# Full-width tiles in a gated linear attention, a bias table written in two steps, and three reorderings around product-key experts

## The reference, cut to what matters

```python
def peer_ffn(h, w_q, sub_keys, expert_u, expert_v):     # 8 heads x 16 experts a token, 2 blocks of 128 tokens
    q = (hb @ w_q).reshape(128, 8, 2, 128)
    s = jnp.einsum('thpc,hpkc->thpk', q, sub_keys)
    top_s, top_i = lax.top_k(s, 16)
    cand_s = top_s[:, :, 0, :, None] + top_s[:, :, 1, None, :]     # 256 candidates
    fin_s, fin_pos = lax.top_k(cand_s.reshape(128, 8, 256), 16)
    idx = take_along_axis(cand_i, fin_pos); gates = softmax(fin_s)
    act = gelu(einsum('thkd,td->thk', expert_u[idx], hb))
    return einsum('thk,thkd->td', gates * act, expert_v[idx])

# second model, layer 0; 4 heads, keys of 96, values of 192
q, k, v, g, lr, mq = split_cols(xn @ gla_w_in, (384, 384, 768, 768, 16, 256))
main = gla_mixer(q, k, v, log_a, g, out_norm)   # ... rmsnorm_2(o, out_norm) * silu(g), per head over its 192
mo = mem_attention(mq, mem_kv)
h = h + concatenate([main, mo]) @ w_out         # 768 + 256 rows
# layer 1: tbl[rel_bucket(dist)], a bias by distance for each of 12 heads
```

## Time and profile before

| | us |
|---|---|
| median of 3 runs | 1646.41 |
| lowest, highest | 1645.17, 1646.71 |
| the profiled execution | 1647.83 |
| its span, first to last instruction | 1646.0 |
| TensorE busy | 1518.2 (92%) |
| VectorE busy | 938.1 (57%) |
| ScalarE busy | 414.1 (25%) |
| GpSimd busy | 597.7 (36%) |

### The profile page before, as it was taken

The page is one execution under the profiler, slowest core; times in us unless marked ns, Lnnn a source line. Parts: engine busy times, 40 slices in busy tenths (PEclk is TensorE's granted clock), DMA queues, the critical chain, the costliest instruction groups (busy, mean ns, idle before and its releaser), DMA issues. The chain is left out here.

```text
span 1646.0 us, 22237 instructions
## 1 busy us (share of the span) xinstructions
PE 1518.2 (92%) x7776; PEld 1138.2 (69%) x7778; DVE 938.1 (57%) x2383; ACT 414.1 (25%) x1007; POOL 597.7 (36%) x524
## 2 busy tenths in 40 slices
PE   7999989999999777778799999999999999999998
PEld 6998845554455323223357788999998878799997
DVE  5652576666766876766454732555553134555554
ACT  2120223213322222222124421111122145311112
POOL 4860233434333444434333103555521000455551
PEclk9999999999999999999999999999999999999999
DMA  8467699999999999999964135654424310555431
GB/s 326 162 224 158 244 428 387 427 426 427 427 420 426 423 427 427 427 426 397 426 282 153 52 128 219 213 169 162 153 106 133 121 52 1 205 169 168 162 127 38
DMA packets 64056, 421.70 MB, mean 256 GB/s; under 512 B 7456, under 2 KB 7904, under 8 KB 18432
## 3 DMA queue, kind: packets, MB, share of 16 engines
q0 software_dynamic: 38944, 277.19, 41.5%
q1 hardware_dynamic: 25024, 143.40, 24.3%
HBM read 416.12 MB, written 3.45 MB: 255 GB/s over the span
## 5 line engine op out<-in xcount | busy, mean ns | idle before, releaser
L2085 PE MATMUL wide<-arena 128*128 128x512 f32 x1024 | 475.4, 611 | 94.9 <-ACT arena L651 94.6
L2085 PEld LDWEIGHTS wide<-arena 128*128 128x128 f32 x1024 | 190.4, 193 | 357.4 <-issue 195.6
L1373 DVE CUSTOM_DVE_ANT_0 arena<-arena,wide 128x1024 f32<-128x1024 f32 x256 | 312.3, 1220 | 175.4 <-DMA arena<-uv_dram,arena 170.5
L494 POOL DMA_INDIRECT arena<-uv_dram,arena x256 | 260.0, 1016 | 406.1 <-PE wide L2085 288.4
L651 ACT ACTIVATE arena<-arena 128x2 f32<-128x2 f32 (+4 forms) x205 | 72.2, 354 | 507.1 <-DVE arena L1373 388.1
L2312 PE MATMUL wide<-arena,wring 128*128 128x256 f32 x704 | 158.6, 379 | 0.0
L1578 DVE SCALAR_TENSOR_TENSOR arena<-arena,prm 128x255 f32<-128x255 f32 (+1 forms) x152 | 126.0, 850 | 55.6 <-ACT arena L651 55.5
L2312 PEld LDWEIGHTS wide<-arena,wring 128*128 128x128 f32 x704 | 130.9, 190 | 16.2
L1612 DVE TENSOR_TENSOR arena<-bank,arena 128x128 f32<-128x128 f32 x266 | 73.9, 290 | 105.1 <-PE bank L2272 101.5
L651 ACT ACTIVATE arena<-bank 128x128 f32<-128x128 f32 (+7 forms) x102 | 41.7, 409 | 347.0 <-PE bank L2272 104.4
L505 POOL TENSOR_TENSOR arena<-arena 128x512 f32<-128x512 f32 x15 | 20.2, 1347 | 298.2 <-ACT arena L651 297.5
(11 more groups left out here) (275 smaller groups left out, 2126.4 us busy)
## 6 DMA issues: line engine op xcount, KB each, us to landing
wring<-ffn_dram SPq DMA_DIRECT2D x44, 1024.0 KB, 5.1
wring<-ffn_dram SPq DMA_DIRECT2D x44, 512.0 KB, 3.5
wring<-win_dram SPq DMA_DIRECT2D x15, 1024.0 KB, 5.4
wring<-wout_dram SPq DMA_DIRECT2D x8, 1024.0 KB, 9.3
wring<-wq_dram SPq DMA_DIRECT2D x5, 1024.0 KB, 7.5
wring<-wout_dram SPq DMA_DIRECT2D x4, 1280.0 KB, 5.5
wring<-mix_dram SPq DMA_DIRECT2D x4, 1024.0 KB, 5.3
arena<-uv_dram,arena POOLq DMA_INDIRECT x256, 11.8
```

What stands on the lines that cost most here:

```text
L494: pool.indirect_dma_start(out=G[:, n % NBUF, :], out_offset=None, in_=a["uv"], in_offset=bass.IndirectOffsetOnAxis(ap=idx[:, u, r:r + 1], ...
L1373: V.tensor_tensor_reduce(out=G[:, n % NBUF, 0:D], in0=G[:, n % NBUF, 0:D], in1=wide[:, 0:2, :].rearrange("p a b -> p (a b)"), scale=1.0, s ...
L2085: ins = MM(wide[:, 2 + h, :], diag[:, n % 4, e, :], G[:, r % NBUF, D + 512 * h:D + 512 * (h + 1)], start=r % (HEADS * TOPK) == 0, stop=r % ...
```

## The change

Six edits in one.

- Tiles. Queries and keys are packed as 3 slots of 2 x 128 columns: tile h holds head h's 96 and 32 of the fourth head's; VectorE copies the fourth head's parts to their partitions (for `gla_qk0` in two operations ahead of its scaling, for the others in four after the scans), and `gla_p0` waits for VectorE's copies. Values and gates are reordered as 4 tiles with the first 128 of each head and 2 tiles that hold the last 64 of two heads each. `glag` has 3 slots, `wout0` 8 row tiles instead of 10, and `gla_v0` stands ahead of `gla_p0`. The roots of the mean squares go from PSUM to `rinv` (ScalarE), the reciprocal is taken there.
- `wout0` runs the first four row tiles over all four groups, then the rest group by group.
- The bias table is written 8 times over (of 128) and copied on in memory by a second transfer; GpSimd waits for three.
- `wout` waits for the mixed tiles one by one.
- Unit 0's index is decoded in two halves (`select_in_halves`), and gathers 0 to 7 wait for the first only.
- `exps(1)` goes to pair 5 of unit 0, `exps(2)` ahead of `keep_head`, `exps(u + 2)` ahead of the eviction in a unit's last pair; some evictions move a pair later.

```diff
-          ("memkv", 4, 2048), ("glalr", 1, 128), ("glaqk", 4, 1536), ("glamq", 1, 2048), ("glav", 2, 3072), ("glag", 4, 1536),
-          ("wout0", 4, 2560), ("ffn0", FT, 3072), ("kvc", 2, 2048), ("nsamq", 1, 2048), ("nsagl", 1, 288), ("nsaq", 3, 2048), ("kvs", 4, 2048),
+          ("memkv", 4, 2048), ("glalr", 1, 128), ("glaqk", 3, 2048), ("glamq", 1, 2048), ("glav", 2, 3072), ("glag", 3, 2048),
+          ("wout0", 4, 2048), ("ffn0", FT, 3072), ("kvc", 2, 2048), ("nsamq", 1, 2048), ("nsagl", 1, 288), ("nsaq", 3, 2048), ("kvs", 4, 2048),
...
-          ("gla_gate", 2, ACT_), ("mean_fin", 1, DVE_), ("gla_qk1", 3, ACT_), ("gla_p0", 2, DVE_), ("gla_v0", 1, ACT_), ("gla_mq", 1, ACT_), ("gla_p1", 2, DVE_),
+          ("gla_gate", 2, ACT_), ("mean_fin", 1, DVE_), ("gla_qk1", 2, DVE_), ("gla_v0", 1, ACT_), ("gla_p0", 2, DVE_), ("gla_mq", 1, ACT_), ("gla_p1", 2, DVE_),
...
-          ("gla_ms", 2, DVE_), ("gla_g2", 1, ACT_), ("gla_g3", 1, ACT_), ("wout0", 4, DVE_),
+          ("gla_ms", 2, ACT_), ("gla_g2", 1, ACT_), ("wout0", 4, DVE_),
...
-                pool.wait_ge(idx_ready, u + 1)
+                pool.wait_ge(idx_ready, u + 2 if u else 1)
...
+                    if n == TOPK // 2:
+                        pool.wait_ge(idx_ready, 2)
+                        pool.sem_inc(fence["pool"])
...
-            pool.dma_start(a["turned"],
-                           tb[:, 512:896].unsqueeze(1).broadcast_to([12, 128, 384])).then_inc(bias_dram, 16)
+            pool.dma_start(a["turned"][:, 0:8, :], tb[:, 512:896].unsqueeze(1).broadcast_to([12, 8, 384])).then_inc(bias_dram, 16)
...
+            turned = a["turned"].tensor
+            pool.dma_start(bass.AP(turned, 8 * 384, [[128 * 384, 12], [8 * 384, 15], [1, 8 * 384]]),
+                           bass.AP(turned, 0, [[128 * 384, 12], [0, 15], [1, 8 * 384]])).then_inc(bias_dram, 16)
+            pool.wait_ge(bias_dram, 48)
...
+                    exps(2)
+                elif u == 1 and p == 2:
...
-                    exps(2)
-                elif 1 <= u <= 4 and p == 4:
+                elif 1 <= u <= 4 and p == 5:
...
+                    if u == 0 and p == 5:
+                        exps(1)
+                    elif u and p == PAIRS - 1 and u + 2 < UNITS:
+                        exps(u + 2)
...
-                if u + 2 < UNITS:
-                    exps(u + 2 if u else 1)
...
-            copy(gq[:, 2:4, :], halves(full("gla_qk1", 0), DK), scale=float(DK) ** -0.5).then_inc(freed[ACT_], 1)
-            copy(gk[:, 0:2, :], halves(full("gla_qk1", 1), DK)).then_inc(freed[ACT_], 1)
+            b = full("gla_qk1", 0)
+            copy(gq[:, 2, :], b[0:DK, 0:S], scale=float(DK) ** -0.5)
+            copy(gk[:, 0, :], b[0:DK, S:2 * S]).then_inc(qk_kept, 1)
+            copy(gk[:, 1:3, :], halves(full("gla_qk1", 1), DK)).then_inc(qk_kept, 1)
...
+            keep_v(0)
...
-            copy(gk[:, 2:4, :], halves(full("gla_qk1", 2), DK)).then_inc(freed[ACT_], 1)
...
-            keep_v(0)
...
-                copy(sqC[0:DK, 4 * n:4 * n + 4, :], wide[0:DK, 2 * n:2 * n + 2, :].rearrange("p a (b t) -> p (a b) t", b=2),
+                copy(sqC[:, 4 * n:4 * n + 4, :], wide[:, 2 * n:2 * n + 2, :].rearrange("p a (b t) -> p (a b) t", b=2),
...
-                root("gla_ms", i, DK, 2 * S)
+                copy(rinv.rearrange("p (q i) t -> p i q t", i=2)[:, i], halves(full("gla_ms", i)), func=ACT.Sqrt, bias=eps[:]).then_inc(freed[ACT_], 1)
...
-            keep_g(3)
...
+            def decode(q):
+                e = slice(8 * q, 8 * q + 8)
+                oh = [onehot[:, p, :].rearrange("p (k i) -> p k i", k=16)[:, e, :] for p in range(2)]
+                steps(V.tensor_scalar(pij[:, 0, e], pos[:, e], 4, 15, ALU.logical_shift_right, ALU.bitwise_and))
+                steps(V.tensor_scalar(pij[:, 1, e], pos[:, e], 15, 15, ALU.bitwise_and, ALU.bitwise_and))
+                join()
+                for p in range(2):
+                    steps(V.tensor_tensor(oh[p], pij[:, p, e].unsqueeze(2).broadcast_to([128, 8, 16]),
+                                          C("iota", 16).unsqueeze(1).broadcast_to([128, 8, 16]), ALU.is_equal))
+                join()
+                for p in range(2):
+                    steps(V.tensor_tensor(oh[p], oh[p], tif[:, p, :].unsqueeze(1).broadcast_to([128, 8, 16]), ALU.mult))
+                join()
+                for p in range(2):
+                    steps(V.tensor_reduce(eij[:, p, e], oh[p], X, ALU.add))
+                join()
+                V.scalar_tensor_tensor(out=idx[:, 0, e], in0=eij[:, 0, e], scalar=float(NKEYS), in1=eij[:, 1, e],
+                                       op0=ALU.mult, op1=ALU.add).then_inc(idx_ready, 1)
+            def select_in_halves():
+                for step in range(5):
+                    select(0, step)
+                flat, flat_w = cand.rearrange("p a b -> p (a b)"), cw.rearrange("p a b -> p (a b)")
+                join()
+                steps(V.max_index(pos[:, 0:8], fs[:, 0, 0:8], flat))
+                join()
+                decode(0)
+                steps(V.match_replace(flat_w, fs[:, 0, 0:8], flat, -3.0e38))
+                select(0, 6)
+                select(0, 7)
+                join()
+                decode(1)
...
-            for step in range(13):
-                select(0, step)
+            select_in_halves()
...
+            for m in range(2):
+                V.scalar_tensor_tensor(out=gq[32 * m:32 * m + 32, 3, :], in0=b[DK:128, m * S:(m + 1) * S], scalar=float(DK) ** -0.5,
+                                       in1=rstd[DK:128, :], op0=ALU.mult, op1=ALU.mult)
...
+            b = full("gla_qk1", 0)
+            dve.wait_ge(qk_kept, 1)
+            V.tensor_scalar(gq[64:DK, 3, :], b[DK:128, 0:S], float(DK) ** -0.5, None, ALU.mult)
+            V.tensor_copy(gk[0:32, 3, :], b[DK:128, S:2 * S]).then_inc(freed[DVE_], 1)
+            b = full("gla_qk1", 1)
+            dve.wait_ge(qk_kept, 2)
+            V.tensor_copy(gk[32:64, 3, :], b[DK:128, 0:S])
+            V.tensor_copy(gk[64:DK, 3, :], b[DK:128, S:2 * S]).then_inc(freed[DVE_], 1)
...
-                    dve.wait_ge(freed[ACT_], TAKEN[GROUP0["gla_qk1"] + 2])
+                    dve.wait_ge(freed[DVE_], TAKEN[GROUP0["gla_qk1"] + 1])
...
-                b = full("gla_ms", h // 2)
-                if h % 2 == 0:
-                    norm.n += 1
-                    dve.wait_ge(rooted, norm.n)
-                steps(V.reciprocal(rinv[:, h, :], b[0:DK, (h % 2) * S:(h % 2 + 1) * S]))
+                lo = 64 * (h % 2)
+                dve.wait_ge(freed[ACT_], TAKEN[GROUP0["gla_ms"] + h % 2])
+                steps(V.reciprocal(rinv[:, h, :], rinv[:, h, :]))
...
-                steps(V.tensor_tensor(gout[:, 2 * h:2 * h + 2, :], wide[0:DK, h, :].rearrange("p (b t) -> p b t", b=2),
-                                      rinv[:, h, :].unsqueeze(1).broadcast_to([DK, 2, S]), ALU.mult))
-                if h % 2:
-                    dve.drain().then_inc(freed[DVE_], 1)
-            steps.join()
-            for h in range(GH):
-                dve.wait_ge(freed[ACT_], TAKEN[GROUP0[f"gla_g{h}"]])
-                for v in range(2):
-                    j = 2 * h + v
-                    ins = V.scalar_tensor_tensor(out=gout[:, j, :], in0=gout[:, j, :], scalar=P("out_norm", v, rows=DK),
-                                                 in1=gg[:, j, :], op0=ALU.mult, op1=ALU.mult)
-                ins.then_inc(g_out, 1)
+                steps(V.tensor_tensor(gout[:, h, :], wide[:, h, 0:S], rinv[:, h, :], ALU.mult))
+                steps(V.tensor_tensor(gout[lo:lo + 64, 4 + h // 2, :], wide[lo:lo + 64, h, S:2 * S], rinv[lo:lo + 64, h, :], ALU.mult))
+                dve.wait_ge(freed[ACT_], TAKEN[GROUP0[f"gla_g{h // 2}"]])
+                steps.join()
+                V.scalar_tensor_tensor(out=gout[:, h, :], in0=gout[:, h, :], scalar=P("out_norm", 0), in1=gg[:, h, :],
+                                       op0=ALU.mult, op1=ALU.mult).then_inc(g_out, 1)
+            dve.wait_ge(freed[ACT_], TAKEN[GROUP0["gla_g2"]])
+            for j in range(4, 6):
+                V.scalar_tensor_tensor(out=gout[:, j, :], in0=gout[:, j, :], scalar=P("out_norm", 1), in1=gg[:, j, :],
+                                       op0=ALU.mult, op1=ALU.mult).then_inc(g_out, 1)
...
-            pe.wait_ge(mixed, 8)
-            def tokens(w, src, b, t, ms=(0, 1), norms=None):
+            def tokens(w, src, b, t, ms=(0, 1), norms=None, mixes=False):
...
+                        if mixes and m == 0:
+                            pe.wait_ge(mixed, k + 1)
...
-                done(tokens(slot("wout", i), mT, b, 0))
+                done(tokens(slot("wout", i), mT, b, 0, mixes=i == 0))
...
-                    lead("gla_qk0", b, slot("glaqk", 0), DK, p // 2 - 1, 0)
+                    lead("gla_qk0", b, slot("glaqk", 0), 128, p // 2 - 1, 0)
...
-                ins = lead("gla_qk0", bank[GROUP0["gla_qk0"] % 4], slot("glaqk", 0), DK, m, 1)
```

(69 more changed lines are left out.)

31 lines of the change are left out of this document (17 added, 14 removed).

## The result

| us | before | after |
|---|---|---|
| median of 7 runs each, taken together | 1646.71 | 1635.61 |
| lowest, highest | 1645.17, 1657.36 | 1631.17, 1637.11 |
| the profiled execution | 1647.83 | 1635.63 |
| its span | 1646.0 | 1633.8 |

The ratio is 0.9899, 95% interval 0.9872 to 0.9926: 1.0%, or 17 us (12 to 21) of the time before. By the medians the gain is 11.1 us, by the profiled executions 12.2. Forecast were 23.6 us and 1622.8 us. The sign and the mechanism were right; the size was not. The median of 1635.61 lies 5 us above the stated range; by the ratio, on the 1646.41 us that the forecast started from, it is 1629.8, just inside it.

A forecast was written before the change was run, and what follows sets the result against it. Transfers were taken to set the pace during the experts' gathers, TensorE afterwards. The terms -4.2 - 0.8 - 2.8 + 0.6 - 16.4 gave -23.6 us, so 1622.8 us from the 1646.41 median, range 1616.5 to 1630.5.

The forecast's parts named there:

- Part A: Lead-in: two-step bias table saves 2.33 us TensorE gap plus 1.83 us half clock, 4.2 us, between 0 and 4.2.
- the covered copy: Lead-in: the bias table's copy in memory takes 6 to 15 us, ending before `wout` needs its weights.
- Part B: Start of the experts: unit 0 decoded in halves, first index 2.3 us sooner, about 0.8 us gained.
- Part C: Experts: exponentials ahead of evictions end VectorE's wait after unit 0, gaining 2.8 us, between 0 and 3.9.
- the price of the table loads: ScalarE, pair 5 of unit 0: moved exponentials cost two table loads of 1.28 us and 0.5, 3.06 us in all.
- Part D: Layer 0's attention: full tiles need fewer instructions, 20.7 us less; with the added waits and savings, 16.4 us less in all.
- `mean_squares` keeps its count: Means of squares ahead of `wout0`: instruction count unchanged, so no time charged.
- counts decide: Attention matmuls: duration does not fall with fewer rows, so 3 x 32 fewer instructions at 0.216 us save 20.7 us.
- the ring moves by two slots, which nothing after it notices: Weight slots after layer 0's attention: shifted by two, with no cost to later work.
- Little from the lead-in and the experts: Rival: A to C give 2 us instead of 7.2, time about 1628; chance 0.15.
- the slow copy: Rival, lead-in: bias table's copy in memory becomes the new wait; chance 0.03 of slower, 0.02 of cancelling the gain.
- Slower: Whole kernel: the changed kernel loses more than 0.2%, 3.3 us; chance 0.04.

The follow-up runs named there:

- A alone: Kernel before with only the bias table written out in two steps: 1649.99 us, ratio 0.9966.
- after_mixed: Changed kernel with all narrow matmuls of layer 1's start put among wide ones: 1624.91 us, ratio 0.9836.
- after_order: Changed kernel with the fourth slot's matmuls last in layer 0's output projection and mean-square matmuls grouped by row count: 1627.85 us, ratio 0.984.
- the two mixed kernels: Changed kernel and kernel before, both with layer 1's narrow matmuls put among wide ones: 1624.91 us and 1647.66 us.
- the interleaved kernel: Changed kernel with the compression's hidden layer interleaved with layer 1's first query projection: 1628.94 us, ratio 0.9861.

## Why the prediction was right, and where it was wrong

**Part A, right.** The gap, the clock, the covered copy (12.2 us, inside 6 to 15) and the folds came as written. At the first gather A alone is 4.3 us ahead (61.86 us from the rows' issue, 66.12 before), the forecast 4.2. By the experts' end it is 5.2, outside the bounds of 0 to 4.2, but by less than the scatter of 1.2 us.

**Part B, right here, wrong alone.** The first index is combined at 177.58, 2.5 us after the search's end at 175.12 (the working had about 2.7). The gain of 0.8 was wrong in place: an earlier gather isn't idle queue time won when the next wait of its consumer stands still. `finish_half` came late as feared: TensorE waits 2.87 us for it (0.83 before), and the clock is 0.69 in 180 to 185.

**Part C, right.** 2.4 of 2.8 us, the mechanism and the price of the table loads as written.

**Part D, terms right, two of them incomplete.** Differences of starts in the two traces:

| stretch | before | after | difference | forecast |
|---|---|---|---|---|
| `mean_fin` to `gla_qk1` | 2.04 | 2.96 | +0.9 | +0.8 |
| `gla_qk1` to first gates | 77.30 | 70.82 | -6.5 | -7.6 |
| first gates to `wout0` | 36.33 | 31.10 | -5.2 | -6.9 |
| `wout0` to feed-forward | 34.77 | 32.16 | -2.6 | -2.7 |

The second lacks 1.1 us: the 64 `gla_qk1` instructions took 16.9 us from start to start, where two of the experiments have 13.9, with clock 0.54 in 860 to 865, after the 1.83 us of waiting ahead of them, while before lost only some 1.6 there. The same wait is followed by full clock in those two (`after_mixed`, `after_order`), so this too differs from one execution to the next. The third lacks 1.7 us: "`mean_squares` keeps its count" was costed at nothing, but its rows went from 96 throughout to 128 and 64 in turn, and the same 16 instructions take 4.92 us for 3.46. So the step "counts decide" was too broad: counts decide where the shape stays the same from one instruction to the next. The fourth is right in both halves, 2.39 us of gap and some 2.1 of half clock (32.16 - 27.63 - 2.39). But that second half was luck: in the mixed kernel the same gap, there 2.44 us, is followed by full clock. With full clock at both places part D is worth 16.6 us between the two mixed kernels (148.83 and 132.20 us from `mean_fin` to the feed-forward), against 16.4 forecast; the sum comes out because the 1.5 us of alternation that it left out and the 1.8 us of half clock that it charged cancel.

**The step that failed.** Up to 992.66 us the forecast had 23.6 us and the trace has 21.6, of which 0.7 is the earlier lead-in: 2.7 short, all of it accounted for in D's second and third stretch. The rest of the miss, 9.4 us, is behind it, where the working had no term. The sum was made against one execution and carried everything after the change over unchanged ("the ring moves by two slots, which nothing after it notices"). That execution had TensorE's full clock in the compression, and so, by their times, had the three runs shown and a third of all runs of the kernel before. The range had no place for losing it. Added up over all windows of 5 us as (1 - clock) x 5, the profiled executions lost 19 us to the clock before and 30.6 after. Of the difference of 11.6 us, 8.5 lie between 1200 and 1300 us, where the kernel before lost nothing. That the total is so near the distance between 12.2 and 23.6 proves nothing: the windows count where TensorE is idle too, and the alternation is no matter of the clock. The seven runs of after lie at 1631.2 to 1632.3 and 1635.6 to 1637.1. Only one was seen, of the second group, and 1635.6 less 7.7 is 1627.9, so all seven may have had the low clock; but the interleaved kernel, with full clock there in its trace, has a run at 1632.1, so the first group may not have had it. Whether the changed kernel is more prone to it than the kernel before stays open: even none of 7, against 4 of 7 low times of the kernel before beside it and 22 of 71 in all, would be too few. With the orders mended, one of four runs came at 1621.4, 6 us under its next.

**The rivals.** None of them happened. "Little from the lead-in and the experts" is refuted by the table above (7.5 us, where it had 2), the slow copy by its 12.2 us. Slower was right to be held small. What was missing was a rival of the kind "the same work at the other clock", worth 8 us, with a chance of about two in three by the runs of the kernel before taken later, and not readable from three runs of 1645.2 to 1646.7.
